# One-hot gate products in fp32r, 256 columns wide, with the two halves added by VectorE

## The reference, cut to what matters

```python
    v1, i1 = lax.top_k(s1, PEER_TOPK)
    v2, i2 = lax.top_k(s2, PEER_TOPK)
    cand = (v1[..., :, None] + v2[..., None, :]).reshape(T, PEER_HEADS, PEER_TOPK * PEER_TOPK)
    sc, pos = lax.top_k(cand, PEER_TOPK)
    e1 = jnp.take_along_axis(i1, pos // PEER_TOPK, axis=-1)
    e2 = jnp.take_along_axis(i2, pos % PEER_TOPK, axis=-1)
    experts = (e1 * PEER_NKEYS + e2).reshape(T, PEER_HEADS * PEER_TOPK)
    gates = jax.nn.softmax(sc, axis=-1).reshape(T, PEER_HEADS * PEER_TOPK)
    ...
        u = peer_u[ec]
        a = jax.nn.gelu(jnp.einsum("ckd,cd->ck", u, hc).astype(jnp.float32)) * gc
        vv = peer_v[ec]
        return jnp.einsum("ck,ckd->cd", a.astype(vv.dtype), vv)
```

## Time and profile before

| | |
|---|---|
| median of 3 runs | 2862.53 us |
| the profiled execution | 2861.7 us |
| its span (first to last instruction) | 2859.8 us |
| PE busy | 2754.3 us, 96% |
| DVE busy | 2224.7 us, 78% |
| ACT busy | 1459.4 us, 51% |
| mean granted clock of PE | 0.986 |
| up phase, about | 1690 to 2309 us of the span |

### The profile page before, as it was taken

The page is one execution under the profiler, slowest core; times in us unless marked ns, Lnnn a source line. Parts: engine busy times, 40 slices in busy tenths (PEclk is TensorE's granted clock), DMA queues, the critical chain, the costliest instruction groups (busy, mean ns, idle before and its releaser), DMA issues.

```text
span 2859.8 us, 37083 instructions
## 1 busy us (share of the span) xinstructions
PE 2754.3 (96%) x13531; PEld 2317.7 (81%) x13531; DVE 2224.7 (78%) x3019; ACT 1459.4 (51%) x1956; POOL 630.7 (22%) x507
## 2 busy tenths in 40 slices
PE   5989969999999999999999999999999999999998
PEld 4767848888888768777787899999999988888887
DVE  7576658888888863888864899999777668888886
ACT  4344238888888744554543334566666533333332
POOL 0321111111111100000020000334333324444442
PEclk7999979999999999999999999999999999999999
DMA  8754539999999733333343234789988999999995
GB/s 319 238 198 160 184 130 348 372 369 367 359 357 360 290 123 123 103 120 102 128 148 128 97 132 166 285 305 327 342 322 309 321 357 362 353 360 357 364 361 174
DMA packets 201723, 738.01 MB, mean 258 GB/s; under 512 B 24352, under 2 KB 77728, under 8 KB 144960
## 3 DMA queue, kind: packets, MB, share of 16 engines
q1 hardware_dynamic: 124656, 497.12, 48.1%
q0 software_dynamic: 55008, 170.98, 17.0%
q10 hardware_dynamic: 21872, 67.48, 6.1%
HBM read 666.61 MB, written 94.04 MB: 266 GB/s over the span
## 4 chain that ended last, share of the span: by engine, by line
PE 61%; DVE 14%; issue 5%; DMA 3%; ACT 2%; POOL 0%; ACTq 0%; DVEq 0%; SPq 0%; POOLq 0%
PE PS L548 54%; DVE wlo L1950 3%; PE PS L1183 2%; DMA ht<-in_peer_v_dram,IDX 1%; PE PS L861 1%; PE PS L1060 1%; DVE hf L2757 1%; ACT whi L1259 1%; DVE oh L2743 1%; DVE zo L2480 1%; DVE hf L2769 1%; ACT HH L1920 1%; DVE cand L2704 1%; DVE cand L2706 1%; PE PS L1046 1%
## 5 line engine op out<-in xcount | busy, mean ns | idle before, releaser
L1950 DVE TENSOR_TENSOR wlo<-raw,whi 128x2048 fp32r<-128x2048 f32 x392 | 894.4, 2289 | 270.8 <-ACT whi L1259 251.1
L1259 ACT ACTIVATE whi<-raw 128x2048 fp32r<-128x2048 f32 x392 | 751.0, 1917 | 356.3 <-PE PS L548 303.9
L548 PE MATMUL PS<-HH,whi 128*128 128x512 f32 (+1 forms) x2064 | 783.5, 380 | 10.2 <-DVE HL L2003 4.3
L548 PE MATMUL PS<-HH,wlo 128*128 128x512 f32 (+1 forms) x2064 | 750.4, 364 | 0.0
L548 PE MATMUL PS<-HL,whi 128*128 128x512 f32 (+1 forms) x2064 | 750.0, 363 | 0.0
L548 PEld LDWEIGHTS PS<-HH,whi 128*128 128x128 f32 x2064 | 389.2, 189 | 65.0 <-issue 14.5
L548 PEld LDWEIGHTS PS<-HL,whi 128*128 128x128 f32 x2064 | 389.7, 189 | 44.5 <-issue 5.5
L548 PEld LDWEIGHTS PS<-HH,wlo 128*128 128x128 f32 x2064 | 388.6, 188 | 42.9
L548 PE MATMUL PS<-whi,HH 128*128 128x512 f32 x864 | 341.6, 395 | 13.7 <-DVE HL L2801 8.3
L548 PE MATMUL PS<-wlo,HH 128*128 128x512 f32 x864 | 338.0, 391 | 0.0
L548 PE MATMUL PS<-whi,HL 128*128 128x512 f32 x864 | 338.0, 391 | 0.0
(11 more groups left out here) (456 smaller groups left out, 3830.5 us busy)
## 6 DMA issues: line engine op xcount, KB each, us to landing
raw<-in_moe_dram SPq DMA_DIRECT2D x192, 1024.0 KB, 7.3
raw<-in_u_units_dram SPq DMA_DIRECT2D x64, 1024.0 KB, 6.2
raw<-in_v_units_dram SPq DMA_DIRECT2D x64, 1024.0 KB, 8.9
raw<-in_w_in_dram SPq DMA_DIRECT2D x44, 1024.0 KB, 5.2
raw<-in_w_ada_dram SPq DMA_DIRECT2D x24, 1024.0 KB, 6.7
acts_dram<-sS ACTq DMA_DIRECT2D x64, 384.0 KB, 5.8
gates_dram<-XT ACTq DMA_DIRECT2D x24, 1024.0 KB, 8.0
sS<-acts_dram SPq DMA_DIRECT2D x42, 384.0 KB, 6.9
```

Of the source, the lines that this page charges most:

```text
L548: ins = t.matmul(dst, a, b, start=(first and n == 0), stop=(last and n == 2))
L1259: a.inc(a.e.activation(m.whi[p % HRING][:, :, :], m.raw[RAW_SLOT[load_of(p)]][:, :, :], ACT.Copy), "hi", p)
L1950: v.inc(v.e.tensor_tensor(m.wlo[h][:, :, :], m.raw[RAW_SLOT[load_of(p)]][:, :, :], m.whi[h][:, :, :].bitcast(F32), ALU.subtract), "lo_v", p)
```

## The change

The weighted one-hot changes its role and its type. Before, the gates scale one one-hot, and an fp32 product multiplies two operands of 128 columns. After, each gate is split into a high part rounded to fp32r (`gh`, by ACT) and the rest (`glo`, by DVE). ACT writes eight scaled copies instead of four: for each of four tokens the second one-hot times the high part, and beside it times the low part, into 256 columns of `HH` or `HL` (their first 128 tokens, which the up phase doesn't read). PE then runs four fp32r products of 256 columns, with the unscaled one-hot as weights, into two banks (4 and 5 or 6 and 7) instead of one of three. ACT copies the first halves to `XT`, and DVE adds the second halves to it (a new instruction, 128x512, out of PSUM), which is now the event `gput`.

The order changes too. PE's step runs the products ahead of the transposes, and the transposes wait for `gput` of group step-6. `oh` has 3 buffers, and DVE's comparison of group g waits for the products of group g-3. The scaled copies of group g wait for the products of g-2, the products of g for the add of g-2. The copy out of PSUM comes at step g+6, as does the add. The DMA is issued by ACT at the start of step g+7. The plan counts 1500 ns instead of 1150 for a gate step on DVE, which moves choice steps to later rows.

```diff
@@ peer_schedule
             tensor += 1100
-            vector += 1150
+            vector += 1500
@@ Plan
-                self.oh = sb(s2, "oh", [128, 4, 2, 4, 128])
+                self.oh = sb(s2, "oh", [128, 3, 2, 4, 128], F32R)
+                self.gh = sb(s2, "gh", [128, 2, 128], F32R)
+                self.glo = sb(s2, "glo", [128, 2, 128])
@@ pe_gate_step
+    n = step - 5
+    if 0 <= n < N_GATE:
+        pe.wait_ge("weighted", n)
+        if n % 32 == 28:
+            pe.wait_ge("eT", min(TD // 128 + n // 32 + 1, NT - 1))
+        if n > 1:
+            pe.wait_ge("gput", n - 2)
+        for k in range(4):
+            ins = t.matmul(m.PS[:, 4 + 2 * (n % 2) + k // 2, 256 * (k % 2):256 * (k % 2) + 256], m.oh[:, n % 3, 0, k, :],
+                           (m.HH, m.HL)[n % 2][:, 2 * k:2 * k + 2, 0:TD], start=True, stop=True)
+        pe.inc(ins, "gmm", n)
     if r == 0 and i < NT:
...
-            pe.wait_ge("eT", i - 1)
+            pe.wait_ge("gput", n - 1)
...
-    n = step - 5
-    if 0 <= n < N_GATE:
-        pe.wait_ge("weighted", n)
-        if n > 2:
-            pe.wait_ge("gput", n - 3)
-        for k in range(4):
-            ins = t.matmul(m.PS[:, 5 + n % 3, 128 * k:128 * k + 128], m.oh[:, n % 4, 0, k, :],
-                           m.oh[:, n % 4, 1, k, :], start=True, stop=True)
-        pe.inc(ins, "gmm", n)
@@ act_gate_step
     n = step - 7
-    if n >= 0:
+    if n >= 0 and n % 4 == 3:
+        tg, w = n // 4, (n // 4) % 2
+        a.wait_ge("gput", n)
+        a.dma(s.dma_start(m.GD[tg, :, :], bass.AP(m.XT, 2048 * w, [[KC * T, 128], [1, 2048]])),
+              f"gate5_out{w}", tg)
+    n = step - 6
+    if 0 <= n < N_GATE:
         tg, w = n // 4, (n // 4) % 2
         a.wait_ge("gmm", n)
...
-                           bass.AP(m.PS, 512 * (5 + n % 3), [[4096, 128], [1, 128], [128, 4]]), ACT.Copy),
-              "gput", n)
...
+                           bass.AP(m.PS, 2048 + 1024 * (n % 2), [[4096, 128], [1, 128], [256, 4]]), ACT.Copy),
+              "ghalf", n)
-    if r == 1 and i < NT:
+    if r == 0 and i < NT:
...
+        a.own()
+        if k > 1:
+            a.wait_ge("gmm", 32 * (k - 1) - 1)
+        a.inc(s.activation(m.gh[:, k % 2, :], m.eT[k % 2][:, 256:384], ACT.Copy), "ghi", i)
     n = step - 3
...
-        a.wait_ge("eT", TD // 128 + k)
+        a.wait_ge("glow", TD // 128 + k)
+        if n > 1:
+            a.wait_ge("gmm", n - 2)
...
-            a.inc(s.activation(m.oh[:, n % 4, 0, j, :], m.oh[:, n % 4, 0, j, :], ACT.Copy,
-                               scale=m.eT[k % 2][:, t:t + 1]), "weighted_part" if j < 3 else "weighted", n)
+            t = 4 * q + j
+            for half, part in enumerate((m.gh[:, k % 2, t:t + 1].bitcast(F32), m.glo[:, k % 2, t:t + 1])):
+                a.inc(s.activation((m.HH, m.HL)[n % 2][:, 2 * j + half, 0:TD], m.oh[:, n % 3, 1, j, :].bitcast(F32), ACT.Copy, scale=part),
+                      "weighted" if j == 3 and half else "weighted_part", n)
@@ dve_gate_step
+    i, r = TD // 128 + step // 32, step % 32
+    if r == 1 and i < NT:
...
+        v.wait_ge("ghi", i)
+        v.inc(v.e.tensor_tensor(m.glo[:, k % 2, :], m.eT[k % 2][:, 256:384], m.gh[:, k % 2, :].bitcast(F32),
+                                ALU.subtract), "glow", i)
+    n = step - 6
+    if 0 <= n < N_GATE:
...
+        v.wait_ge("ghalf", n)
+        dst = bass.AP(m.XT, 2048 * w + 4 * (n % 4), [[KC * T, 128], [16, 128], [1, 4]])
+        v.inc(v.e.tensor_tensor(dst, dst, bass.AP(m.PS, o + 128, [[4096, 128], [1, 128], [256, 4]]), ALU.add), "gput", n)
     n = step - 2
...
-        if n > 3:
-            v.wait_ge("gmm", n - 4)
+        if n > 2:
+            v.wait_ge("gmm", n - 3)
```

More of the change, by code:

```diff
@@ L1874, in act_gate_step @@
         a.wait_ge("onehot", n)
-        a.wait_ge("eT", TD // 128 + k)
+        a.wait_ge("glow", TD // 128 + k)
+        if n > 1:
+            a.wait_ge("gmm", n - 2)
         for j in range(4):
-            t = 256 + 4 * q + j
-            a.inc(s.activation(m.oh[:, n % 4, 0, j, :], m.oh[:, n % 4, 0, j, :], ACT.Copy,
-                               scale=m.eT[k % 2][:, t:t + 1]), "weighted_part" if j < 3 else "weighted", n)
+            t = 4 * q + j
+            for half, part in enumerate((m.gh[:, k % 2, t:t + 1].bitcast(F32), m.glo[:, k % 2, t:t + 1])):
+                a.inc(s.activation((m.HH, m.HL)[n % 2][:, 2 * j + half, 0:TD], m.oh[:, n % 3, 1, j, :].bitcast(F32), ACT.Copy, scale=part),
+                      "weighted" if j == 3 and half else "weighted_part", n)
 def act_gather_step(a, m, step):
@@ L2733, in dve_gate_step @@
 def dve_gate_step(v, m, step):
+    i, r = TD // 128 + step // 32, step % 32
+    if r == 1 and i < NT:
+        k = i - TD // 128
+        v.wait_ge("ghi", i)
[3 more added lines that the diff above has]
+    if 0 <= n < N_GATE:
+        tg, w, o = n // 4, (n // 4) % 2, 2048 + 1024 * (n % 2)
+        v.wait_ge("ghalf", n)
+        dst = bass.AP(m.XT, 2048 * w + 4 * (n % 4), [[KC * T, 128], [16, 128], [1, 4]])
+        v.inc(v.e.tensor_tensor(dst, dst, bass.AP(m.PS, o + 128, [[4096, 128], [1, 128], [256, 4]]), ALU.add), "gput", n)
     n = step - 2
@@ L2740, in dve_gate_step @@
         v.wait_ge("const5", "io128")
-        if n > 3:
-            v.wait_ge("gmm", n - 4)
-        v.inc(v.e.tensor_tensor(m.oh[:, n % 4, :, :, :],
+        if n > 2:
+            v.wait_ge("gmm", n - 3)
+        v.inc(v.e.tensor_tensor(m.oh[:, n % 3, :, :, :],
                                 bass.AP(m.io128, 0, [[128, 128], [0, 2], [0, 4], [1, 128]]),
```

## The result

| | before | changed |
|---|---|---|
| median | 2863.62 us (5 runs beside it) | 2874.27 us (5 runs, 2871.74 to 2876.25) |
| ratio, 95% interval | | 1.0035 [1.0023, 1.0046] |
| profiled execution, span | 2861.7, 2859.8 us | 2871.7, 2870.0 us |
| DVE busy | 2224.7 us | 2279.8 us |
| mean granted clock of PE | 0.986 | 0.980 |

The change makes the kernel slower, by 0.35%. The forecast was +2.1 us and the profiled execution shows +10.2, inside the range. The forecast's own value lies within 0.2% of before; what came is the "slower" outcome, to which the prediction gave 0.37.

The account below looks back on a forecast made before the run. DVE was taken to bound the up phase's first half, PE the second: +17.7 and -15.6 us, net +2.1 on the profiled 2861.7, giving 2863.8. With 0.9 for the median of runs: 2864.6 us, range 2855 to 2880.

Parts of the forecast that it names:

- PE's saving: Up phase: four 256-column products at 0.120 us each cut a gated row on PE from 5.05 to 4.64 us.
- rival 3: Slower: weight loads pace the 256-column products, row 4.91 us, second half 13.2 us more, 2878 us; chance 0.07.
- rival 4: Slower: the products don't become cheaper, 17.7 us and 4.6 more in the second half, 2885 us; chance 0.02.
- The add: DVE's new 128x512 add out of PSUM: 0.68 us long, counted at 0.60 each, 27.0 for 45 in rows 23 to 67.
- The gathers' DMA wait: Row 22: DVE's gathers, now behind a choice step, no longer wait for their DMA, saving 5.3 us.
- DVE owns the first half: DVE bounds the up phase up to row 67; products of row 68 start 17.7 us later, at 2036.1.
- (a): Row 49: transposes wait for the same row's add, ACT's copies for them; DVE stalls 4.5 us.
- (b): Row 25: tile 0's exp with two table loads lengthens ACT's chain to 8.5 us; DVE stalls 2.2.
- Row 82: Second half: a tile's transposes in row 81 (0.34 us) now wait for the same row's add (1.7).
- The general allowance of 2.5: Second half: 2.5 us for what doesn't fit, as DMA would be busy 98%.
- Rival 2: Slower: ACT the bound, even rows 5.63 us and odd 4.64, 5.14 a row, 2886 us; chance 0.12.
- the signs: Expected profile: rows of 4.64 to 4.70 from row 69, row 68 12 to 22 us later, up phase's end within some 6.

Follow-up runs that it names:

- small add: The changed kernel with DVE's add cut to 4 of 512 columns, leaving most low halves out of the gates: 2847.34 us.
- transposes first: The changed kernel with a tile's transposes ahead of the products, in bank 6, waiting for the add of two groups before: 2866.28 us.
- three buffers: The changed kernel with three buffers for the product groups instead of two, products of group g waiting for the add of g-3: 2871.12 us.
- three buffers, earlier transposes: The changed kernel with three product-group buffers and a tile's transposes waiting for the add of one group earlier: 2861.76 us.
- high halves alone: The kernel before with 1500 in the plan and one 128-column fp32r product per token, low halves left out, no add: 2825.24 us.

## Why the prediction came near, and where it was short

The range held the result, and the mechanism is the one that came. But every size that was off was off in the same direction, and the forecast of +2.1 us is a fifth of what came. In the profiled execution row 68 is 4.3 us later than forecast, the second half gains 1.8 less, and 2.1 more stand behind row 117. The median of the changed kernel is 2.5 us over its profiled execution, where 0.9 had been added. That the end stayed inside is owed to a range of 15 us above the forecast.

**PE's saving: right.** A gated row takes 4.64 us, as worked out from the spacings of 384 and 512 columns. The rival of 0.19 us a load (rival 3) and the one of no saving (rival 4) are out. The second half gained 13.8, not 15.6, mostly because of row 82.

**The add: right.** 0.68 us each, as in the earlier trace rows. Cut to 4 columns it is 0.15 us long and its follower starts some 0.07 behind it, so 45 adds give back about 24 us of DVE's time. 18.9 us of them come back in rows 22 to 68.

**The gathers' DMA wait: right.** DVE waited for no DMA between 1762 and 2032 in the changed kernel, so the 5.3 us taken off did go.

**DVE owns the first half: right, but the ties aren't free.** Rows 22 to 68 and 68 to 117, in us:

| | 22 to 68 | 68 to 117 |
|---|---|---|
| before | 246.45 | 247.97 |
| changed | 268.58 | 234.15 |
| small add | 249.68 | 230.37 |
| transposes first | 266.33 | 230.73 |
| three buffers | 261.76 | 239.63 |
| three buffers, earlier transposes | 257.75 | 233.82 |

The time of the add is the larger part. PE's own waits there mostly cost nothing by themselves: with three buffers one of them goes, the next comes up, and the whole gains 3 us. What does cost is the tie of the transposes to the add of the same row: in the first half it makes DVE itself wait, in the second PE. With it loosened too the kernel is 12.5 us under the changed one by the medians and 11.2 between rows 22 and 117, with DVE's work unchanged. The order of the transposes is 8.0 us (on the changed kernel) or 9.4 (on three buffers) of the medians, not far from the 10.7 that the change lost.

**The stalls: right in place, short in size.** (a) was 5.2 us against 4.5. From the end of the add to the end of ACT's copy it took 7.6 instead of 7.0. PE made the transposes at a granted clock of 0.50, and ACT could start 1.1 us behind the add, where 0.4 had been reckoned. (b) was 4.1 against 2.2. The timeline of DVE:

```profile
1804.44 0.69 DVE L2759 TENSOR_TENSOR XT<-XT,PS 128x512 f32<-128x512 f32 x1 [4.12 <-ACT XT L1868]
```

Together 2.6 of the 4.3 us by which row 68 came later than forecast (2040.4, not 2036.1). The other 1.7 have no single place.

**Row 82: wrong in size.** "Row 81 has a tile's transposes (0.34), which now wait for the add of the same row (1.7)" priced it as 2.0 us. The products of row 82 came 9.44 us behind those of row 81, a loss of 4.8. PE waits 2.88 us for the add before the transposes. It doesn't wait again at its next products; the rest is the transposes and a granted clock of 0.50 from 2106.0 to 2108.6.

```profile
2106.19 0.66 PE L1187 MATMUL PS<-ident,e 128*128 128x128 f32 x2 [2.88 <-DVE XT L2759]
...
2112.12 0.63 PE L1177 MATMUL PS<-HH,oh 128*128 128x256 f32 x4
```

With the transposes earlier this row is 4.97. Rows 73 to 76 lost 1.9 more. The general allowance of 2.5 took up part of both.

**The clock: wrong.** "PE doesn't pause long enough in either half for me to change that" fails in both halves. The granted clock fell to 0.50 behind PE's waits, at rows 49 and 81 among others, and its mean from row 22 to 68 was 0.95. At row 82 it is some 1.6 us of the loss. In the first half DVE sets the pace, so it may have cost little there; no run shows it apart.

**"and so does the down phase": not settled.** The profiled execution is 2.5 us longer there, but its first stretch is as long (42.68 us) in the kernel before with 1500.

**ACT: right that it just fits.** Rival 2 had even rows at 5.63 and odd rows held at 4.64. ACT gave the even rows back in the odd ones: nearly every row from 83 on is 4.64.

**Of the signs** named ahead, the end of the up phase is the one missed: 7.7 us later than before, not within 6. Row 68, 21.9 us later, is at the edge of its 12 to 22.

**Left out: what the rings cost.** The kernel before pays 6 us for them. In the changed kernel this can't be added to the sum, as DVE's time already covers it there.

**Open.** The 21 us between the small add and high halves alone (249.68 and 228.58 in rows 22 to 68) are not shown apart. What would explain them: the small adds still take DVE's time; DVE waits 14.3 us for ACT's copy; ACT makes eight copies instead of four; and with high halves alone the products need only DVE's comparison of three rows earlier, so that PE passes row 68 while DVE is still in row 66. More buffers were tried only with the full add, and the earlier transposes never with the small one.

## What to carry to other kernels

Ask who owns each stage before moving work between engines. Here the second half gave 13.8 us and the first took 21.9, and the mean busy shares (PE 96%, DVE 78%) said the contrary. A consumer inserted between PSUM and its reuse ties PE to that engine's longest rows; look at every place where the order of the new tie closes a circle (here, a tile's transposes, twice), and price each by the same chain. Here that order loosened, with three buffers, brought the changed kernel from 2874.27 to 2861.76 us, level with the kernel before. And try a planner's number by itself: 1500 in the kernel before gives 8 us (2856.33 us against 2864.37) and needs nothing else, and no changed kernel that keeps the low halves was faster; in the changed kernel it made no difference that the scatter lets one see.

## What the runs showed of the hardware

Products of 128 columns in fp32r cost 0.113 us each when every one has its own weights, and of 256 columns 0.120: the second 128 columns are nearly free.

The lower clock stands behind PE's own waits here. After 7.58 us of idle time the four products took 1.20 us, rather than 0.63 (granted clock 0.50 from 1788.8 to 1791.3):

```profile
1788.82 1.20 PE L1177 MATMUL PS<-HH,oh 128*128 128x256 f32 x4 [7.58 <-DVE XT L2759]
```

After 4.79 us, at 1936.05 above, matmuls of 384 columns stand 0.32 apart instead of 0.173. The granted clock is 0.50 from 1935.9 to 1938.5 (the lower of the two levels, 1.2 against 2.4 GHz) and 0.98 from 1938.5 to 1941.0. The first window's mean is 0.96, against 0.99 in the earlier trace rows.
